# The MLP's split matmuls of one kernel: six of 288 columns made into five of up to 384, in three PSUM banks

## What is computed

```
h2 = rmsnorm(x, lp['norm2_g'])
x = x + jnp.square(jax.nn.relu(h2 @ lp['w_up'])) @ lp['w_down']
```

## Time and profile before

| | us |
|---|---|
| median of 3 runs | 2852.74 (2849.63 to 2854.64) |
| the profiled execution's own time | 2851.12 |
| its span | 2849.3 |
| PE busy | 2634.1 (92%) |
| PEld busy | 2427.8 (85%) |
| DVE busy | 1321.5 (46%) |
| ACT busy | 565.6 (20%) |
| POOL busy | 1060.0 (37%) |

### The profile page before, as it was taken

The page is one execution under the profiler, slowest core; times in us unless marked ns, Lnnn a source line. Parts: engine busy times, 40 slices in busy tenths (PEclk is TensorE's granted clock), DMA queues, the critical chain, the costliest instruction groups (busy, mean ns, idle before and its releaser), DMA issues.

```text
span 2849.3 us, 61458 instructions
## 1 busy us (share of the span) xinstructions
PE 2634.1 (92%) x24742; PEld 2427.8 (85%) x24742; DVE 1321.5 (46%) x2272; ACT 565.6 (20%) x1119; POOL 1060.0 (37%) x596
## 2 busy tenths in 40 slices
PE   8878899789998999999998688995999989999998
PEld 7867688479997999999988577873999889999998
DVE  5345786453436531221543468864344466312215
ACT  2011222311113220110210212224111132200112
POOL 3503233012223555555544032320122235555553
PEclk9989899689999999999999798995999999999999
DMA  5201111111124322222231111121111343222221
GB/s 188 83 23 64 44 60 62 70 37 49 60 79 155 128 83 82 89 81 81 85 136 60 38 57 51 53 73 52 48 49 54 135 128 109 81 86 85 81 81 70
DMA packets 66727, 222.79 MB, mean 78 GB/s; under 512 B 8256, under 2 KB 9024, under 8 KB 65472
## 3 DMA queue, kind: packets, MB, share of 16 engines
q1 hardware_dynamic: 45360, 160.59, 16.6%
q10 hardware_dynamic: 21136, 58.84, 6.0%
HBM read 190.38 MB, written 29.03 MB: 77 GB/s over the span
## 4 chain that ended last, share of the span: by engine, by line
PE 80%; DVE 9%; DVEq 5%; issue 3%; ACT 2%; ACTq 1%; DMA 0%
PE dense L494 64%; PE mix L494 14%; DVEq L1423 4%; DVE region_b L1670 1%; PE mix L897 1%; ACT region_b L1000 1%; DVE region_b L1762 1%; ACT in_hi L1000 0%; DVE region_b L1820 0%; DVE region_b L1773 0%; DVE act_lo L1885 0%; PE mix L593 0%; DVE x L1714 0%; DVE region_b L1459 0%; DVE x L1672 0%
## 5 line engine op out<-in xcount | busy, mean ns | idle before, releaser
L478 POOL TENSOR_SCALAR w_hi<-w_raw 128x1024 fp32r<-128x1024 f32 x296 | 312.6, 1056 | 1742.4 <-PE dense L494 1412.5
L481 POOL TENSOR_TENSOR w_lo<-w_raw,w_hi 128x1024 fp32r<-128x1024 f32 x296 | 747.3, 2525 | 24.6
L494 PE MATMUL dense<-act_hi,w_hi 128*128 128x288 f32 x2272 | 689.6, 314 | 17.2 <-DVE act_lo L1441 13.6
L494 PE MATMUL dense<-in_hi,w_hi 128*128 128x288 f32 x2432 | 678.7, 294 | 10.4 <-DVE in_lo L1875 8.8
L494 PE MATMUL dense<-in_lo,w_hi 128*128 128x288 f32 x2432 | 678.4, 295 | 0.0
L494 PE MATMUL dense<-act_lo,w_hi 128*128 128x288 f32 x2272 | 652.2, 298 | 0.0
L494 PE MATMUL dense<-act_hi,w_lo 128*128 128x288 f32 x2272 | 534.9, 296 | 0.0
L494 PE MATMUL dense<-in_hi,w_lo 128*128 128x288 f32 x2432 | 521.9, 296 | 0.0
L494 PEld LDWEIGHTS dense<-act_hi,w_hi 128*128 128x128 f32 x2272 | 434.2, 191 | 74.3 <-issue 44.6
L494 PEld LDWEIGHTS dense<-in_hi,w_hi 128*128 128x128 f32 x2432 | 458.6, 189 | 12.5 <-issue 9.1
L494 PEld LDWEIGHTS dense<-in_lo,w_hi 128*128 128x128 f32 x2432 | 458.9, 189 | 0.0
(11 more groups left out here) (192 smaller groups left out, 2625.6 us busy)
## 6 DMA issues: line engine op xcount, KB each, us to landing
w_raw<-in_stream SPq DMA_DIRECT2D x296, 512.0 KB, 3.2
y_mix<-gate_scratch ACTq DMA_DIRECT2D x48, 288.0 KB, 2.9
gate_scratch<-region_b ACTq DMA_DIRECT2D x36, 288.0 KB, 3.0
x_scratch<-x ACTq DMA_DIRECT2D x2, 2304.0 KB, 12.5
y_scratch<-y_mix ACTq DMA_DIRECT2D x2, 2304.0 KB, 8.0
x<-x_scratch ACTq DMA_DIRECT2D x2, 2304.0 KB, 9.9
y_mix<-y_scratch ACTq DMA_DIRECT2D x2, 2304.0 KB, 9.2
gate_scratch<-region_a ACTq DMA_DIRECT2D x12, 288.0 KB, 2.1
```

What stands on the lines that cost most here:

```text
L478: nc.gpsimd.tensor_scalar(w_hi[:, v, :], w_raw[:, s, :], 1.0, 1.0, ALU.mult, ALU.mult).then_inc(w_high, 1)
L481: nc.gpsimd.tensor_tensor(w_lo[:, v, :], w_raw[:, s, :], w_hi[:, v, :].bitcast(F32), ALU.subtract).then_inc(w_split, 1)
L494: return nc.tensor.matmul(out, lhsT, rhs, start=start, stop=stop, skip_group_check=True)
```

## The change

The MLP's tiles get a function of their own, mlp_tile. in_hi and in_lo become the two halves of one buffer in_hl, so that high and low parts of a slice lie side by side as 1152 columns. The high weights multiply these in three matmuls of 384 columns, each into a bank of its own, and the low weights multiply the 576 high columns in one matmul of 384 (into the first bank) and one of 192 (into the second). So a slice has five matmuls with five weight loads. The product with the low activations stays in PSUM words of its own, and DVE adds the two parts as they leave PSUM: in an up tile by two copies and two adds, then the maximum and the factor from SBUF; in a down tile by four adds to x. A tile takes three banks; the two sets are banks 0 to 2 and 5 to 7, and the sum of squares of the MLP's norm goes to banks 3 and 4. PE waits ahead of the first MLP tile for both dense pairs, since its banks cover parts of both. In sum_squares both waits now stand ahead of the first matmul. All other dense tiles stay as they are.

```diff
--- before.py
+++ after.py
@@ -212,8 +212,8 @@
 
         with nc.sbuf_tensor("region_b", [P, WORDS_B], F32) as region_b:
             pass
-        in_hi = sb("in_hi", [P, 16, T], F32R)
-        in_lo = sb("in_lo", [P, 16, T], F32R)
+        in_hl = sb("in_hl", [P, 16, 2 * T], F32R)
+        in_hi, in_lo = in_hl[:, :, 0:T], in_hl[:, :, T:2 * T]
         ra = region_a
 
         class Carve:
@@ -321,8 +321,13 @@
         relu_m = yret[:, 0:2, :]
         sq_m = yret[:, 2:4, :]
 
-        dense = [ctx.enter_context(nc.psum_tensor(f"dense{i}", [P, 1024], F32)) for i in range(2)]
-        mix = [ctx.enter_context(nc.psum_tensor(f"mix{i}", [P, 1024], F32)) for i in range(2)]
+        banks = ctx.enter_context(nc.psum_tensor("banks", [P, 4096], F32))
+        dense = [banks[:, 1024 * i:1024 * i + 1024] for i in range(2)]
+        mix = [banks[:, 2048 + 1024 * i:3072 + 1024 * i] for i in range(2)]
+
+        third = 2 * T // 3
+        mlp_banks = [banks[:, 0:1536], banks[:, 2560:4096]]
+        mlp_sums = banks[:, 1536:2560]
 
         r_ps, y_ps, z_ps = (dense[1][:, 256 * i:256 * i + 256] for i in range(3))
         u_ps = r_ps
@@ -519,6 +524,23 @@
                         fresh(k)
                     mm = dense_slice(buf, slot, hi, lo, half * ks + k, k0 + k, k == 0, k == ks - 1)
                 mm.then_inc(w_used, used)
+
+            def mlp_tile(m, split_count, free_count, k0, fresh):
+
+
+                buf = mlp_banks[m % 2]
+                pe.wait_ge(w_split, split_count)
+                pe.wait_ge(dense_free[m % 2], free_count)
+                for k in range(KT):
+                    if fresh:
+                        fresh(k)
+                    wh, wl = (w[:, m % SPLIT, k * P:k * P + P] for w in (w_hi, w_lo))
+                    for i in range(3):
+                        acc(buf[:, 512 * i:512 * i + third], wh, in_hl[:, k0 + k, third * i:third * i + third],
+                            k == 0, i == 2 and k == KT - 1)
+                    acc(buf[:, 0:third], wl, in_hl[:, k0 + k, 0:third], False, k == KT - 1)
+                    mm = acc(buf[:, 512:512 + T - third], wl, in_hl[:, k0 + k, third:T], False, k == KT - 1)
+                mm.then_inc(w_used, 2)
 
             def tile(l, t, u, hi, lo, **kw):
                 dense_tile(t % SPLIT, u % 2, l * NT + t + 1, free_before(u, l), hi, lo,
@@ -559,12 +581,12 @@
                     if k == KT - 1:
                         mm.then_inc(w_used, 3 if half and t == T_SPARE - 1 else 1)
 
-            def sum_squares(n):
+            def sum_squares(n, sums):
 
                 pe.wait_ge(sq_summed, n * (KT - 2) + KT - 2)
-                wide(mix[0], ones, n_sum, T, True, False)
                 pe.wait_ge(sq_ready, n * KT + KT)
-                wide(mix[0], ones, n_sq[:, 1, :], T, False, True).then_inc(ssq_ready, 1)
+                wide(sums, ones, n_sum, T, True, False)
+                wide(sums, ones, n_sq[:, 1, :], T, False, True).then_inc(ssq_ready, 1)
 
             def rotate(l, n, mat, src):
 
@@ -796,7 +818,7 @@
                     tile(l, T_RET + t, T_RET + t, act_hi, act_lo, fresh=fresh)
                     if t == 0:
                         pe.wait_ge(in_const, 32)
-                        sum_squares(l * 2)
+                        sum_squares(l * 2, mix[0])
                     if 1 <= t <= 8:
                         rotate(l, t - 1, rot_ret, t_raw)
                 for i in range(4):
@@ -983,15 +1005,17 @@
                             fresh = lambda k: pe.wait_ge(act_ready, l * (2 * KT) + (KT + k + 1))
                         if m == KT:
                             fresh = lambda k: pe.wait_ge(mlp_split, START + l * (FF * KT) + c * KT + k + 1)
-                        dense_tile(m % SPLIT, m % 2, l * NT + T_MLP + c * (2 * KT) + m + 1,
-                                   free_before(U_MLP + m, l) + c * KT, in_hi, in_lo, k0=0 if up else KT, fresh=fresh)
                         if first and m == 0:
-                            sum_squares(l * 2 + 1)
+                            pe.wait_ge(dense_free[1], free_before(U_MLP + 1, l))
+                        mlp_tile(m, l * NT + T_MLP + c * (2 * KT) + m + 1, free_before(U_MLP + m, l) + c * KT,
+                                 0 if up else KT, fresh)
+                        if first and m == 0:
+                            sum_squares(l * 2 + 1, mlp_sums)
 
                 mlp_chunk(0, True)
                 with pe.Fori(1, FF) as c:
                     mlp_chunk(c)
-            sum_squares(2 * DEPTH)
+            sum_squares(2 * DEPTH, mix[0])
 
 
         @block.scalar
@@ -1022,9 +1046,9 @@
                 nc.scalar.drain()
                 return op(out, out, ACT.Exp, scale=-0.5)
 
-            def norm_root(n):
+            def norm_root(n, sums):
                 act.wait_ge(ssq_ready, n + 1)
-                root(n_rs, mix[0], T, 1.0 / D, 0).then_inc(rs_ready, 1)
+                root(n_rs, sums, T, 1.0 / D, 0).then_inc(rs_ready, 1)
 
             def after_dve(l, u0):
 
@@ -1158,7 +1182,7 @@
             act.wait_ge(in_const, 32)
             with act.Fori(0, DEPTH) as l:
                 act.dma_start(r_tab, dr["r_tab"]).then_inc(in_ret, 16)
-                norm_root(l * 2)
+                norm_root(l * 2, mix[0])
                 act.dma_start(r_con, dr["r_con"]).then_inc(in_con, 16)
                 act.dma_start(st_s[:, :, :], layer_of(dr["st_ret"], l).rearrange("p (h e) -> p h e", e=P)).then_inc(in_con, 16)
                 act.dma_start(x_dram, x[:, :, :]).then_inc(x_away, 16)
@@ -1396,7 +1420,7 @@
                         merged_high(n // 6 - 1)
                 merged_high(3)
                 squares(l * 2 + 1, after_dve(l, U_WO), in_hi, "g2")
-                norm_root(l * 2 + 1)
+                norm_root(l * 2 + 1, mlp_sums)
                 act.wait_ge(act_ready, l * (2 * KT) + 2 * KT)
                 act.dma_start(par[:, 0:NPAR], dr["par"][bass.ds(l + 1, 1), :, :].rearrange("a p n -> p (a n)")).then_inc(in_par, 16)
                 with act.Fori(0, FF) as c:
@@ -1410,7 +1434,7 @@
                         nc.scalar.drain()
                         op(in_hi[:, KT + m, :], sq_m[:, m % 2, :], ACT.Copy).then_inc(mlp_act, 1)
                 squares(l * 2 + 2, after_dve(l, U_MLP + (FF - 1) * 2 * KT + KT), act_hi, "g1", l * 16 + 32)
-            norm_root(2 * DEPTH)
+            norm_root(2 * DEPTH, mix[0])
             act.wait_ge(out_stored, DEPTH * OUTS)
 
 
@@ -1441,14 +1465,36 @@
                 v.scalar_tensor_tensor(lo[:, k, :], x[:, k, :], pr(gain, k), hi[:, k, :].bitcast(F32), ALU.mult,
                                        ALU.subtract).then_inc(act_ready, 1)
 
+            def low_thirds(m):
+
+
+
+                edge = 512 + T - third
+                return (mlp_banks[m % 2][:, edge:edge + 640].rearrange("p (a b) -> p a b", b=320)[:, :, 0:third // 2],
+                        mlp_banks[m % 2][:, 1024 + third // 2:1024 + third])
+
+            def mlp_add(m):
+
+                buf, (rest, rest_end) = mlp_banks[m % 2], low_thirds(m)
+                first, end = x[:, m, 0:third], x[:, m, third:T]
+                in_two = first.rearrange("p (a b) -> p a b", b=third // 2)
+                v.tensor_tensor(first, first, buf[:, 0:third], ALU.add)
+                v.tensor_tensor(end, end, buf[:, 512:512 + T - third], ALU.add)
+                settle()
+                v.tensor_tensor(in_two, in_two, rest, ALU.add)
+                v.tensor_tensor(end, end, rest_end, ALU.add).then_inc(dense_free[m % 2], 1)
+
             def residual(l, n, m, t, buffer, hi, lo, gain):
 
                 if m:
                     sum_square(n, m - 1)
                     low_part(n, m - 1, hi, lo, gain)
                 dve.wait_ge(w_used, used_after(t, l))
-                v.tensor_tensor(halves(x[:, m, :]), halves(x[:, m, :]), out_of(dense[buffer]),
-                                ALU.add).then_inc(dense_free[buffer], 1)
+                if buffer is None:
+                    mlp_add(m)
+                else:
+                    v.tensor_tensor(halves(x[:, m, :]), halves(x[:, m, :]), out_of(dense[buffer]),
+                                    ALU.add).then_inc(dense_free[buffer], 1)
                 if m == KT - 1:
                     settle()
                     low_part(n, m, hi, lo, gain)
@@ -1922,10 +1968,15 @@
                         dve.wait_ge(w_used, used_after(T_MLP + m, l) + c * (4 * KT))
                         if m >= 2:
                             dve.wait_ge(mlp_sq, l * (FF * KT) + c * KT + (m - 1))
-                        v.scalar_tensor_tensor(halves(relu_m[:, m % 2, :]), out_of(dense[m % 2]), 0.0, halves(n_rs), ALU.max,
-                                               ALU.mult).then_inc(dense_free[m % 2], 1)
-                        dve.wait_ge(dense_free[m % 2], free_before(U_MLP + m, l, 1) + c * KT)
-                        dve.sem_inc(mlp_relu, 1)
+                        buf, (rest, rest_end), up = mlp_banks[m % 2], low_thirds(m), relu_m[:, m % 2, :]
```

(13 more changed lines are left out.)

## The result

The changed kernel takes 2885.0 us (median of 4 runs, 2882.0 to 2887.6) against 2853.7 for the one before: ratio 1.0112, 95% interval 1.0094 to 1.0129, 31 us slower. The forecast was 2874. The profiled execution's span is 2882.1 us, 32.8 more than before.

What follows compares the result with a forecast made beforehand. The prediction took PE's unbroken MLP matmuls as the bound. Slices +8, chunk changes +10.4, starts +2 and end +2 made +22.4 us on 2851.1, say 2874 (forecast band 2865 to 2883, chance 0.40; range 2835 to 2908).

Steps and rivals of the forecast that it cites:

- excess with the columns: Rival for PE's MLP slices: a matmul's cost beyond streaming grows with its columns, 813 ns a slice, 2889 us; chance 0.22.
- PE's slice: MLP matmuls on PE: four of 171.7 ns plus one of 111, 798 ns a slice, +8 us over 1024 slices.
- fixed excess: MLP matmuls on PE: each pays 11.7 ns beside its columns whatever their number, so 384 columns take 171.7 ns.
- The change from up to down: In each of 8 chunks, DVE's take-out waits for POOL's w_lo and PE waits 1.3 us before slice 7: +10.4 us.
- The MLP's start: At each of two MLP starts, PE waits for DVE's add of w_o's last tile: 1.0 us each, +2.0 us.
- The end: End of run: longer last add to x, 1.0 us, and half the sum of squares behind the last square, 1.05: +2.0 us.
- short matmul at f32's rate: Rival for PE's slices: 192 fp32r columns stream like f32, 322 ns, slice 1009 ns, 3079 us; chance 0.12.
- faster case: Rival for PE's slices: the excess vanishes for long matmuls, slice 759 ns, -32 us, 2835 us; chance 0.10.
- load-bound one: Rival for PE's slices: fp32r weight loads need 131.7 ns, 384 columns take 162, slice 779 ns, 2855 us; chance 0.10.
- No wait for POOL: Rival at the chunk changes: DVE's take-out isn't shut out by POOL, so they cost nothing, 2863 us; chance 0.06.

Runs made afterwards that it cites:

- experiment 1: The changed kernel with the norm's factor for the MLP written into PSUM, so the take-out's last operation has one SBUF input: 2873.3 us, ratio 1.0068.
- Experiment 2: The changed kernel with other PSUM banks for the MLP, dropping PE's wait before its first tile and letting half the final sum run early: 2878.4 us, ratio 1.0085.
- experiment 3: The kernel before with its MLP's halves cut at 384 and 192 columns instead of 288 and 288, no added DVE work: 2924.2 us, ratio 1.0246.

## Why the prediction was right or wrong

The direction and the mechanisms held, the order of their sizes did not: the slices, forecast as the second term, were the largest. The time, 2885, lies 2 us above the band that the forecast was given (2865 to 2883) and below the rival "excess with the columns" (2889), whose view of a matmul's cost is the one that came true.

- *PE's slice*: +8 us forecast, +17.0 found. The step that failed is "I take 171.7 and 111": the load was right (108 measured for an estimated 111), the 384 columns were not. They take 174.6, near the upper end of 175.6, for the excess over the streaming goes almost wholly with the columns. 288, 384 and 512 columns at 131.7, 174.6 and about 231 ns lie on 3 ns + 0.446 ns a column. I chose the fixed excess because it lay in the middle; the f32 rows, which show nearly no excess at half the column rate, spoke for the other and I read them as the rival's only. This is 9 of the 11 us by which the forecast fell short.
- *The change from up to down*: 10.4 forecast, 10.8 found, and experiment 1 shows the cause. Counted from DVE's start, the last operation came at 1.81 (forecast 1.84), ended at 4.31 (4.30), and slice 7's low part was done at 6.66 (6.67).
- *The MLP's start*: 1.0 each forecast, 1.3 found. Ahead of the first matmul after the wait the chain has 0.32 us of issue, which I left out.
- *The end*: 2.0 forecast, 3.3 found. The sum's two terms came; what I missed is the clock at 0.62 after PE's 2.69 us of idleness, 3.57 - 2.11 = some 1.4 us on eight matmuls. Experiment 2, where the clock stays at 1.00, gives it back.
- *Rivals*: the short matmul at f32's rate (322 ns for 192 columns) is refuted by the 108 ns of the changed kernel and of experiment 3. The faster case and the load-bound one fall with 384 columns at 174.6. "No wait for POOL" falls with the 2.44 us of the take-out's last operation. The Trainium skill ("TensorE: Matmul & The Clock Gate", "Back-to-back issue gap") has N / 2.4 + 2.5 ns as the gap of an isolated matmul; by that rule it would be 162.5 ns for 384 columns and 215.8 for 512, the traces have 174.6 and 231. The prediction's word that the rule agrees for f32's wide matmuls is too kind: those have 512 columns and are 0.43 us apart, twice what the rule says, and only the excess beside their streaming is as small. What the Trainium skill says on the lock between DVE and GpSimd ("SBUF — State Buffer", "Who interferes with whom") was borne out by experiment 1: 0.75 us in the midst of w_lo with one SBUF input, against an end 0.62 us behind w_lo with two.
- *Open*: why fp32r's columns take 0.446 ns at a granted clock of 1.00, where at 0.50 show one cycle of 1.2 GHz a column and nothing beside; and why parts that no edit touches move by 1 to 3 us from one program to the next. At the change of layers it is the length of PE's idle stretch and the clock behind it, as shown above; the +1.8 us ahead of layer 0's MLP I have not traced.

## What to carry to other kernels

Where PE runs without a break, count columns and hidden loads, not matmuls: joining matmuls of the same columns gained nothing, and one matmul shorter than its weight load cost 108 ns for 80 ns of streaming. Before an operation is split or moved from PSUM to SBUF operands, look what POOL does at that moment: the second SBUF input, not the extra operations, made the stall, and placing one operand in PSUM removed it. A wait that is moved ahead of work that used to fill a gap costs the time of that work and can, as at this kernel's end, cost the clock too.

## What the runs showed of the hardware that I had not expected

- fp32r matmuls with 128 x 128 weights at a granted clock of 1.00: 64 and 192 columns 108 to 111 ns, 288 columns 131.7, 384 columns 174.6 (177 on average in two other sequences), 512 columns 230 to 234. The two short widths cost a weight load.
- The same 288 columns read as bfloat16 four bytes apart: 127.2 ns.
- Eight f32 matmuls after 2.69 us without PE work took 3.57 us at a mean granted clock of 0.62; in experiment 2, with four of them done ahead and a gap of 1.55 us, the clock stayed at 1.00.
- A DVE operation of 576 columns with two SBUF inputs that started within POOL's w_lo ended 0.61 to 0.62 us after it, 62 times of 62.
